# Splitting the norms between the stages of a two-layer diffusion backbone into a context and a latent half

## What is computed

```python
def rmsnorm(x, g, eps=1e-6):
    y = x * lax.rsqrt(jnp.mean(x * x, axis=-1, keepdims=True) + eps)
    return y * g
def modulate(h, shift, scale):
    return h * (1.0 + scale) + shift
def ffn_sublayer(s, m, g_norm, w_in, w_out):
    h = modulate(rmsnorm(s, g_norm), m[0], m[1])
    return s + FFN_RES * m[2] * swiglu(h, w_in, w_out)
```

## Time and profile before

| | us |
|---|---|
| median of three runs | 2678.47 (2675.43 to 2680.24) |
| profiled execution | 2672.84 |
| its span | 2671.2 |
| TensorE busy | 2470.2 (92%) |
| VectorE busy | 1386.2 (52%) |
| ScalarE busy | 868.1 (32%) |
| POOL busy | 395.3 (15%) |
| mean granted TensorE clock | 0.953 |

### The profile page before, as it was taken

How to read it: one execution, slowest core, us unless ns; L and a number is a source line. 1 busy time by engine, 2 the same in 40 slices (tenths; PEclk the granted TensorE clock), 3 DMA queues, 4 the chain that set the end, 5 groups by cost and what they waited for, 6 DMA issues and landing times.

```text
span 2671.2 us, 36686 instructions
## 1 busy us (share of the span) xinstructions
PE 2470.2 (92%) x13996; PEld 2092.2 (78%) x13996; DVE 1386.2 (52%) x2291; ACT 868.1 (32%) x1303; POOL 395.3 (15%) x372
## 2 busy tenths in 40 slices
PE   4999999989989898989999999999998888888998
PEld 4788787976668786778888788888787687867998
DVE  4778875414443434478773355542344534336554
ACT  1533223233421214252222343322343412125553
POOL 2000131001131311300101100001001223122001
PEclk9999999989989999999999899999798988979999
DMA  5455554111110104345553344433231101024555
GB/s 225 145 195 194 185 165 138 56 56 48 60 48 13 48 25 150 111 160 193 190 190 94 94 149 142 141 104 93 95 111 48 63 20 50 1 83 150 181 174 149
DMA packets 96457, 302.82 MB, mean 113 GB/s; under 512 B 10592, under 2 KB 17504, under 8 KB 95584
## 3 DMA queue, kind: packets, MB, share of 16 engines
q1 hardware_dynamic: 76912, 229.69, 25.9%
q0 software_dynamic: 18720, 69.21, 7.6%
q10 hardware_dynamic: 720, 2.44, 0.2%
HBM read 290.81 MB, written 10.49 MB: 113 GB/s over the span
## 4 chain that ended last, share of the span: by engine, by line
PE 85%; DVE 5%; POOL 3%; ACT 3%; issue 2%; DMA 1%; ACTq 0%; DVEq 0%; SPq 0%; POOLq 0%
PE ps L1450 21%; PE ps L1452 20%; PE ps L1451 20%; PE ps L1719 3%; PE ps L1728 3%; PE ps L1735 2%; PE ps L1626 2%; PE ps L1647 1%; PE ps L1558 1%; ACT buf_b L658 1%; PE ps L1416 1%; PE ps L1773 1%; PE ps L1774 1%; POOL w_lo L519 1%; PE ps L1569 1%
## 5 line engine op out<-in xcount | busy, mean ns | idle before, releaser
L1450 PE MATMUL ps<-h_hi,w_hi 128*128 128x512 f32 (+1 forms) x2000 | 745.8, 373 | 46.5 <-DVE h_lo L990 26.8
L1451 PE MATMUL ps<-h_lo,w_hi 128*128 128x512 f32 (+1 forms) x2000 | 727.7, 364 | 0.0
L1452 PE MATMUL ps<-h_hi,w_lo 128*128 128x512 f32 (+1 forms) x2000 | 726.8, 363 | 0.0
L998 DVE TENSOR_TENSOR w_lo<-raw,w_hi 128x1024 fp32r<-128x1024 f32 (+2 forms) x368 | 416.4, 1136 | 464.5 <-ACT w_hi L626 460.6
L626 ACT ACTIVATE w_hi<-raw 128x1024 fp32r<-128x1024 f32 (+2 forms) x416 | 404.6, 974 | 680.2 <-DMA raw<-in_w_down 315.4
L1450 PEld LDWEIGHTS ps<-h_hi,w_hi 128*128 128x128 f32 x2000 | 386.6, 193 | 123.2 <-issue 35.0
L1452 PEld LDWEIGHTS ps<-h_hi,w_lo 128*128 128x128 f32 x2000 | 386.7, 193 | 57.7
L1451 PEld LDWEIGHTS ps<-h_lo,w_hi 128*128 128x128 f32 x2000 | 387.5, 194 | 54.0
L1450 PE MATMUL ps<-a_hi,w_hi 128*128 128x512 f32 (+1 forms) x960 | 347.6, 362 | 28.0 <-DVE a_lo L1360 15.3
L1452 PE MATMUL ps<-a_hi,w_lo 128*128 128x512 f32 (+1 forms) x960 | 349.3, 364 | 0.0
L1451 PE MATMUL ps<-a_lo,w_hi 128*128 128x512 f32 (+1 forms) x960 | 347.4, 362 | 0.0
(11 more groups left out here) (200 smaller groups left out, 2706.9 us busy)
## 6 DMA issues: line engine op xcount, KB each, us to landing
raw<-in_w_up SPq DMA_DIRECT2D x176, 512.0 KB, 4.0
ada<-in_w_ada_t POOLq DMA_DIRECT2D x128, 512.0 KB, 4.2
raw<-in_w_down SPq DMA_DIRECT2D x64, 384.0 KB, 3.1
raw<-in_w_gate SPq DMA_DIRECT2D x48, 512.0 KB, 3.6
raw<-in_w_down SPq DMA_DIRECT2D x64, 320.0 KB, 2.9
raw<-in_w_proj SPq DMA_DIRECT2D x32, 512.0 KB, 3.5
raw<-in_w_merge SPq DMA_DIRECT2D x16, 512.0 KB, 3.5
raw<-in_w_out SPq DMA_DIRECT2D x16, 512.0 KB, 3.5
```

The costliest lines, as they stand in the source:

```text
L998: vec.tensor_tensor(w_lo[:, j % RING, 0:cols], raw[:, j, 0:cols], w_hi[:, j % RING, 0:cols].bitcast(F32), ALU.subtract).then_inc(s_lo, 1)
L1450: pe.matmul(out, wh, rows_hi[:, i, 0:n], start=first, stop=False)
L1451: pe.matmul(out, wh, rows_lo[:, i, 0:n], start=False, stop=False)
L1452: return pe.matmul(out, wl, rows_hi[:, i, 0:n], start=False, stop=last)
```

## The change

**Norms 1 to 4** (`NORM_PARTS` is 2) are done in two parts: part 0 is the context half, part 1 the latent half. Each has its own sums, root, reciprocal and spread (banks 6 and 7). `split_norm` replaces the body of `norm` on ScalarE and VectorE. In it ScalarE issues `shift(p, k + 1)` ahead of `upper(p, k)`, and the rounding and lowering of blocks 0 to 3 stand inside part 0. TensorE's sums and spreads are placed between products (`part_sums`, `part_spread`).

**The end of the stage before** is split too. In feed-forwards 0 to 2 the last down block is multiplied for the context half first (bank 5), then for the latent half (bank 4), whose four chunks alone are counted in `s_pe`. In the first mixer output blocks 5, 6 and 7 are multiplied for the context, then for the latent tokens.

**The first four blocks** of stages 1 to 4 are multiplied by `first_four`: blocks 0 and 1 for the context half, tile by tile with block 1 two tiles behind; then blocks 2 and 3 for the context half; then the same for the latent half. In the mixers these four blocks lie in banks 0 to 3, and `ba` follows them.

**The mixers' projections 7 to 9** use `dense` like the others; their results are copied to `prob` and `probT`, transposed by TensorE into banks 2 to 4 and copied once more (`take_tokens`). The loops on ScalarE and VectorE round and lower blocks from 4 on.

The diff, cut to its core (counters that move from `s` to `part(s)`, new semaphores and unchanged context lines are left out):

```diff
+SPLIT_STAGES = (1, 2, 3, 4)
+NORM_PARTS = (1, 2, 2, 2, 2, 1, 1)
+SPLIT_OUT = 5
...
+def proj_bank(n):
+    return n if n < RING else n % 2
+def out_bank(k, p):
+    return ((5, 0, 1), (2, 3, 4))[p][k - SPLIT_OUT]
...
+    def split_norm(s, l, which):
+        shifted = [0] * KD
+        def weights(j):
+            landed(j, STAGE_BASE[s])
+            cast(j).then_inc(s_hi, 1)
+        def last_square(p):
+            c = part_cols(s, p, TOK)
+            act.wait_ge(*(tile_ready(s, KD - 1) if p else context_ready(s)))
+            act.activation(buf_b[:, 1, c], x[:, KD - 1, c], ACT.Square).then_inc(s_sq, 1)
+        def root(p):
+            t = part_tiles(s, p, TOK)
+            act.wait_ge(s_sum, part(s, p) + 1)
+            act.activation(rms[:, t], ps[:, 6 + p, t], ACT.Sqrt, bias=eps_col[:, 0:1],
+                           scale=1.0 / D).then_inc(s_rt, 1)
+        def shift(p, k):
+            c = part_cols(s, p, TOK)
+            act.wait_ge(s_t, KD * part(s, p) + k + 1)
+            if k >= 2:
+                act.wait_ge(s_h, KD * part(s, p) + k - 1)
+            chain[0] += 1
+            shifted[k] = chain[0]
+            act.activation(buf_b[:, k % 2, c], buf_a[:, k % 2, c], ACT.Identity,
+                           bias=mod[:, l, 3 * which * KD + k, 1 - p:2 - p],
+                           scale=gain[:, l, which, k, 1 - p:2 - p]).then_inc(s_act, 1)
+        def upper(p, k):
+            c = part_cols(s, p, TOK)
+            act.wait_ge(s_act, shifted[k])
+            act.activation(h_hi[:, k, c], buf_b[:, k % 2, c], ACT.Copy).then_inc(s_hhi, 1)
+        last_square(0)
+        root(0)
+        act.wait_ge(s_mods, mods_at(l, which))
+        shift(0, 0)
+        for k in range(KD):
+            if k + 1 < KD:
+                shift(0, k + 1)
+            upper(0, k)
+            if k == 0:
+                weights(0)
+            if k == 2:
+                last_square(1)
+                weights(1)
+            if k == 4:
+                root(1)
+            if k == 5:
+                weights(2)
+        weights(3)
+        shift(1, 0)
+        for k in range(KD):
+            if k + 1 < KD:
+                shift(1, k + 1)
+            upper(1, k)
...
             act.wait_ge(s_pe, b0 + n + 1)
-            bank = ps[:, n % 2, :]
...
                                      bank.rearrange("p (s n) -> p s n", s=2), ACT.Copy)
             elif n == 6:
                 ins = act.activation(kT[:, :], bank, ACT.Copy)
-            elif n == 7:
-                ins = act.activation(v_nat[:, :, :], bank.rearrange("p (t n) -> p t n", t=TT), ACT.Copy)
             elif n < 10:
-                ins = act.activation(pool_nat[:, 0:no // P, (n - 8) * P:(n - 7) * P],
-                                     bank[:, 0:no].rearrange("p (t n) -> p t n", n=P), ACT.Copy)
+                tok = TOK if n == 7 else no
+                ins = act.activation(channel_rows(n)[:, 0:tok], bank[:, 0:tok], ACT.Copy)
             elif n < 12:
...
+        def take_tokens(n):
+            act.wait_ge(tkt.sem, tkt.at(l, n - 6))
+            tok = TOK if n == 7 else no
+            dst = v_nat[:, :, :] if n == 7 else pool_nat[:, 0:no // P, (n - 8) * P:(n - 7) * P]
+            act.activation(dst, ps[:, n - 5, 0:tok].rearrange("p (t n) -> p t n", n=P),
+                           ACT.Copy).then_inc(tke.sem, 1)
...
-            if n >= 2:
+            if n >= RING:
                 block(n)
+            if 11 <= n < 14:
+                take_tokens(n - 4)
...
+    def split_norm(s):
+        l = s // 4
+        def add_last(p, k, bank, which):
+            c = part_cols(s, p, TOK)
+            return vec.scalar_tensor_tensor(x[:, k, c], ps[:, bank, c],
+                                            mod[:, l, (3 * which + 2) * KD + k, 1 - p:2 - p],
+                                            x[:, k, c], ALU.mult, ALU.add)
+        def add(p, k):
+            if s == 2:
+                if p:
+                    vec.wait_ge(s_pe, MIX_BASE[0] + BRANCH_BLOCK + KD + k + 1)
+                    add_last(p, k, out_bank(k, p), 1).then_inc(outd.sem, 1)
+                else:
+                    vec.wait_ge(outh, k - SPLIT_OUT + 1)
+                    add_last(p, k, out_bank(k, p), 1).then_inc(outc, 1)
+                return
+            f = {1: 0, 3: 1, 4: 2}[s]
+            if p:
+                vec.wait_ge(s_pe, STAGE_BASE[s])
+                add_last(p, k, 4, 2 * (f % 2)).then_inc(s_down, 1)
+            else:
+                vec.wait_ge(s_half, f + 1)
+                add_last(p, k, 5, 2 * (f % 2)).then_inc(s_addc, 1)
+        def inverse(p):
+            t = part_tiles(s, p, TOK)
+            vec.wait_ge(s_rt, part(s, p) + 1)
+            vec.reciprocal(inv[:, t], rms[:, t]).then_inc(s_inv, 1)
+        def scaled(p, k):
+            c = part_cols(s, p, TOK)
+            if k == 0:
+                vec.wait_ge(s_bc, part(s, p) + 1)
+            if k >= 2:
+                vec.wait_ge(s_hhi, KD * part(s, p) + k - 1)
+            vec.tensor_tensor(buf_a[:, k % 2, c], x[:, k, c], ps[:, 6 + p, c], ALU.mult).then_inc(s_t, 1)
+        def rest(p, k):
+            c = part_cols(s, p, TOK)
+            vec.wait_ge(s_hhi, KD * part(s, p) + k + 1)
+            vec.tensor_tensor(h_lo[:, k, c], buf_b[:, k % 2, c], h_hi[:, k, c].bitcast(F32),
+                              ALU.subtract).then_inc(s_h, 1)
+        if s == 2:
+            for k in range(SPLIT_OUT, KD):
+                add(0, k)
+        else:
+            add(0, KD - 1)
+        inverse(0)
+        if s == 2:
+            add(1, SPLIT_OUT)
+        scaled(0, 0)
+        for k in range(KD):
+            if k + 1 < KD:
+                scaled(0, k + 1)
+            rest(0, k)
+            if k == 0:
+                if s == 2:
+                    add(1, SPLIT_OUT + 1)
+                lower(0, STAGE_BASE[s])
+            if k == 2:
+                add(1, KD - 1)
+                lower(1, STAGE_BASE[s] + 1)
+            if k == 4:
+                inverse(1)
+            if k == 5:
+                lower(2, STAGE_BASE[s] + 2)
+        lower(3, STAGE_BASE[s] + 3)
+        scaled(1, 0)
+        for k in range(KD):
+            if k + 1 < KD:
+                scaled(1, k + 1)
+            rest(1, k)
...
         if f < 3:
             modulations((0, 1, 1)[f], (3, 0, 3)[f], (9, 3, 9)[f])
+            return
...
         for n in range(N_PROJ + 2):
-            if n >= 2:
+            if n >= RING:
                 lower(n % RING, b0 + n)
...
+        for i in range(KD if l else SPLIT_OUT):
             vec.wait_ge(s_pe, bo + i + 1)
-            add_to_x(i, 7 * (i % 2), no, l, 1).then_inc(outd.sem, 1)
+            add_to_x(i, 4 + i % 2, no, l, 1).then_inc(outd.sem, 1)
             if i + 2 < KD:
                 lower((i + 2) % RING, bo + i + 2)
+        if l == 0:
+            lower((KD - 1) % RING, bo + KD - 1)
...
+    def part_sums(s, p):
+        t = part_tiles(s, p, TOK)
+        pe.wait_ge(s_acc, part(s, p) + 1)
+        pe.wait_ge(s_sq, part(s, p) + 1)
+        for t in range(t.start, t.stop):
+            cols = slice(t * P, (t + 1) * P)
+            pe.matmul(ps[:, 6 + p, t:t + 1], buf_a[:, 0, cols], ones[:, 0:1], start=True, stop=False)
+            ins = pe.matmul(ps[:, 6 + p, t:t + 1], buf_b[:, 1, cols], ones[:, 0:1], start=False, stop=True)
+        ins.then_inc(s_sum, 1)
...
-    def dense_tokens(j, b, bank, n):
-
-        pe.wait_ge(s_lo, b + 1)
-        for t in range(n // P):
...
+    def first_four(s, b):
+        lag = 2
+        for p in range(2):
+            c = part_cols(s, p, TOK)
+            def product(m, k):
+                return products(ps[:, m, c], h_hi, h_lo, m, k, k, c, k == 0, k == KD - 1)
+            pe.wait_ge(s_lo, b + 1)
+            for k in range(KD + lag):
+                if k < KD:
+                    pe.wait_ge(s_h, KD * part(s, p) + k + 1)
+                    ins = product(0, k)
+                if p and k == KD - 1:
+                    ins.then_inc(s_pe, 1)
+                if k == lag:
+                    pe.wait_ge(s_lo, b + 2)
+                if k >= lag:
+                    ins = product(1, k - lag)
+                if p == 0 and k == 4:
+                    part_sums(s, 1)
+            if p:
+                ins.then_inc(s_pe, 1)
+            else:
+                part_spread(s, 1)
+            for m in range(2, RING):
+                pe.wait_ge(s_lo, b + m + 1)
+                if p == 0 and s == 2:
+                    pe.wait_ge(outd.sem, outd.at(0, KD - 2 + m - 2))
+                for k in range(KD):
+                    ins = product(m, k)
+                if p:
+                    ins.then_inc(s_pe, 1)
...
+        if NORM_PARTS[s] == 2:
+            first_four(s, b0)
+        else:
+            first_two(s, b0, n)
+            up(1, 1)
...
-        with pe.Fori(1, KD // 2) as it:
+        if f == 3:
+            with pe.Fori(1, KD // 2) as it:
+                down(it, 0)
+                down(it, 1)
+            return
```

(61 more changed lines are left out.)

94 lines of the change are left out of this document (67 added, 27 removed).

## The result

The median of four runs is **2729.39 us** (2723.82 to 2729.88), against 2678.58 for four runs of the kernel before; the ratio is 1.0187, interval 1.0173 to 1.0201. The forecast was 2728, range 2704 to 2746. The profiled execution has a span of 2728.0 us and a mean granted clock of 0.938; before it was 2671.2 and 0.953.

A forecast was written before the change was run, and what follows sets the result against it. TensorE's order of work, its products' pace plus its waits, was taken as the bound. Stage losses of 11.6, 11.9, 25.3 and 29.6 less mixer gains of 15.9 and 11.8 made +50.7 us: forecast 2728 us, range 2704 to 2746.

The forecast's parts named there:

- The ring: Split norm: rounding, subtraction, next scaling and shift wait on each other across ScalarE and VectorE, 1.80 us per tile.
- F: Stages 1 to 4: time from the end of the last block's context half to block 3's end, forecast 55.6 us.
- The half clock in the context half: Split norm's context half: sparse TensorE work lets its clock fall to half, costing 3.6 us more per stage.
- T: Zero point of the one-stage layout: the end of the last block's context half.
- `ba`: Small projection after the first four blocks in each mixer, priced at 15.5 us in stage 1 and 15.95 in stage 4.
- Stage 1's context half: Last block's context half in stage 1, delayed by VectorE's late fourth weight chunk, forecast to end at 12.45 us.
- Stage 3: From the last down block's start to block 3's end: 52.4 us before, 64.0 forecast, including 0.5 for block 4's later loads.
- The token projections: Mixer projections 7 to 9 through `dense`: stretches from `ba` to last projection forecast to gain 15.9 and 11.8 us.
- The wait for block 4: Mixers, right after `ba`: TensorE idles 9.1 us while VectorE does two convolutions before block 4's low weights.
- The sum: Four stage losses less the two mixers' gains, forecast as +50.7 us for the whole change.
- The norm keeps pace: Rival for the split norm: a half's tile takes 0.95 us, not 1.80, giving 2667 us; chance of faster 0.05.
- rounding first: Rival case in the split norm: ScalarE rounds before the next shift, about +4 us, 2682; 2682 to 2700 had chance 0.05.

The follow-up runs named there:

- round_first: The changed kernel with ScalarE rounding each tile right behind its shift, before turning to the next tile; 2693.10 us, ratio 1.0070.
- reordered: The changed kernel with rounding right behind each shift, mixer blocks 4 and 5 prepared before the `ba` wait, and other norm work moved; 2636.97 us, ratio 0.9861.
- filled_four: The changed kernel with twelve extra unread 256-column products ahead of TensorE's wait for each context-half tile from the second on; 2724.41 us in one run.
- filled_two: The changed kernel with six extra unread 256-column products ahead of TensorE's wait for each context-half tile from the second on; 2726.01 us, ratio 1.0193.
- tokens_only: The kernel before with only the new token projections (blocks 7 to 9 through `dense`, then transposed); 2647.56 us, ratio 0.9915.

## Why the prediction was right, point by point

- **The ring.** Right, and shown: forecast 1.80 us a tile, measured 1.73 (of its four members only scaling start to shift start is off, 0.44 for 0.51); with ScalarE's order turned round it is 0.94, as in the rows of stage 5. ScalarE sat idle 0.82 us with the shift of the next tile at the head of its queue while the rounding of the last one was ready. By the Trainium skill (TensorE: Matmul & The Clock Gate, Architectural detail), which states strict FIFO for ScalarE, it must; the trace agrees.
- **F.** 55.6 forecast, 54.2 to 56.0 measured. The order in it is shown by round_first. Its first terms hold too: the first scaling of stage 1 at 439.51 is 5.84 us behind the context half's end, forecast 5.8. The placing of the other work inside part 0 (weights, last addition, the latent half's sums and spread, moved together) is shown as a cost by round_first and reordered, 45.6 against 37.6 on average; how much of these 8 us is the weights' alone was not tried.
- **The half clock in the context half.** It fell as forecast, but 3.6 us a stage is too large where it was tested: 1.0 in stage 3 of filled_four, 2.4 and 3.6 in stages 4 and 2 of filled_two. The 55.6 is thus met partly by errors that cancel: in stage 3 the context half's eighth subtraction comes 28.8 us behind T where the layout at full clock has 27.9, the latent half's 46.0 where it has 43.9; with 3.6 for the clock the latter would be 47.5.
- **`ba`.** The step that assumed it unchanged, 15.5 and 15.95 us, was mis-sized: 17.3 and 17.4. The clock falls to half sooner inside it, behind the split stages: in the first mixer 3.3 us into it (at 492.54) instead of 5.3 (at 464.80). It is 3.3 us in all.
- **Stage 1's context half.** 12.45 forecast, 11.96 measured; TensorE waits there twice for `w_lo`, 1.80 and 1.72 us, as VectorE's late chunks let one expect.
- **Stage 3.** 1.9 us too much: block 4 did not come late (0.5), and F was 54.2.
- **The token projections.** The gains of 15.9 and 11.8 are 15.9 and 10.9; in the second mixer 0.6 of the 0.9 missing is a wait for `w_lo` ahead of block 9. By themselves (tokens_only) 14 and 9 us were expected, 13.8 and 8.1 measured. A transpose cost a little less than the 0.12 of the earlier trace rows. The trace of the changed kernel has four of them start from 550.42 on, 0.11 us apart, and the next product at 550.78; each lasts 0.27 us (least, median and greatest duration in ns, all eight on `prob`):

```profile
550.42 0.60 PE L1832 MATMUL ps<-consts,prob 128*128 128x128 f32 x4
550.78 0.47 PE L1686 MATMUL ps<-h_hi,w_hi 128*128 128x512 f32 x1
```
```profile
L1832 PE MATMUL ps<-consts,prob x8: 270/272/273, 550.4 to 2031.4; 128*128 128x128 f32 x8
```

The 275 ns of the Trainium skill (TensorE: Matmul & The Clock Gate, Part 4: PE-mode transpose) is a duration, and the trace agrees with it as that. The prediction's sentence took it for the price of each; since the transposes overlap, the 3 us more did not come.
- **The wait for block 4.** 9.1 forecast, 9.09 in both mixers.
- **The sum.** +50.7 forecast, +51.5 measured over its terms. That the medians differ by 50.8 as well is partly luck. Between the two profiled executions the difference is 56.8: the tail adds 5.6 with nothing changed in it, a term that the forecast lacks, and the profiled execution of the kernel before was 5.7 us below its median while that of the changed kernel was at its median.
- **The rivals.** "The norm keeps pace" had its decision point at F = 43; 45.2 to 46.6 still lost, 36.7 to 39.6 won (there with blocks 4 and 5 early as well, worth 8.4 us; with F alone the sum would still be 50.7 less 4 x 18). The price given for rounding first (F 44, 2682) was 1 to 3 us a stage too low, and the time 11 us.

## What to carry to other kernels

To hide a norm behind products, write down for each tile who waits for whom across both engines before asking whether each engine has time: here both were idle half the time and the ring between them still set the pace, for the sake of one instruction issued a tile too early (38 us). Where the other work stands inside such a ring (weights, the last addition, the other half's sums and spread, moved together) was worth another 32 us; both together are worth 70. Try the parts of a change apart: here one part was a gain of 1%, and the other a loss of 3% in one order and no loss in another.
